# A hybrid decoder trunk on one core: more output units inside the last attention rounds, one query unit moved, row norms broadcast without a diagonal matrix

## What is computed

```python
def rmsnorm(x, g):
    y = x * rsqrt(mean(x * x, axis=-1) + 1e-6)
    return y * g

for i in range(2):
    hn = rmsnorm(x, norm_mix_pre[i])
    m = mamba2_mixer(hn, ...) if i == 0 else diff_attention(hn, ...)
    x = x + rmsnorm(m, norm_mix_post[i])
    hn = rmsnorm(x, norm_ffn_pre[i])
    x = x + rmsnorm(conv_ffn(hn, ...), norm_ffn_post[i])

def diff_attention(u, w_qkv, ..., w_out):      # per head: q, k of 2 x 64, v of 128
    sc = q @ k.T * scale - slope * dist        # causal, two score matrices a head
    a = softmax(sc)[0] - lam * softmax(sc)[1]
    out = rmsnorm(a @ v, subln_g) * (1 - lambda_init)
    return out @ w_out                         # 1024 x 1024
```

## Time and profile before

| | us |
|---|---|
| median of 3 runs | 1522.05 |
| lowest, highest | 1521.98, 1523.62 |
| profiled execution, its own time | 1520.41 |
| its span, first to last instruction | 1518.4 |

### The profile page before, as it was taken

One profiled execution on the slowest core, in us unless ns is written; L12 is line 12 of the kernel. 1 busy time (PEld: TensorE's weight loads), 2 busy tenths in 40 slices (PEclk: granted clock), 3 DMA queues, 4 the chain that ended last, 5 costly groups with the idle time before them and its releaser, 6 DMA issues.

```text
span 1518.4 us, 20441 instructions
## 1 busy us (share of the span) xinstructions
PE 1460.5 (96%) x6774; PEld 1162.1 (77%) x6774; DVE 1021.9 (67%) x1428; ACT 613.2 (40%) x953; POOL 192.4 (13%) x123
## 2 busy tenths in 40 slices
PE   6999999999998999999999999999789999999996
PEld 5778888888786788888888767776568888888885
DVE  6888898889427787778422667778357877776223
ACT  5654555557324323322322436565443332233221
POOL 3011100111113000000011332222121000000111
PEclk9999999999999999999999999999889999999998
DMA  4433323332221222223322121111121322223221
GB/s 150 156 125 124 138 98 137 124 138 70 84 90 63 98 97 86 94 97 105 103 95 86 54 70 56 69 55 55 42 97 56 97 97 97 95 87 112 95 95 55
DMA packets 36277, 142.10 MB, mean 94 GB/s; under 512 B 4048, under 2 KB 4176, under 8 KB 34192
## 3 DMA queue, kind: packets, MB, share of 16 engines
q1 hardware_dynamic: 36240, 141.62, 27.1%
HBM read 139.38 MB, written 2.23 MB: 93 GB/s over the span
## 4 chain that ended last, share of the span: by engine, by line
PE 75%; issue 10%; DVE 7%; POOL 3%; ACT 3%; DMA 1%; DVEq 0%; SPq 0%; POOLq 0%; ACTq 0%
PE bank L395 17%; PE bank L396 16%; PE bank L397 16%; PE b_x L395 6%; PE b_x L397 6%; PE b_x L396 6%; POOL w_lo L350 3%; DVE w_lo L358 1%; DVE cv_s L812 1%; PE b_y L828 1%; ACT w_hi L344 1%; PE b_y L395 1%; PE b_y L396 1%; PE b_y L397 1%; PE b_x L840 1%
## 5 line engine op out<-in xcount | busy, mean ns | idle before, releaser
L358 DVE TENSOR_TENSOR w_lo<-raw,w_hi 128x1024 fp32r<-128x1024 f32 (+1 forms) x190 | 254.4, 1339 | 290.4 <-ACT w_hi L344 290.2
L344 ACT ACTIVATE w_hi<-raw 128x1024 fp32r<-128x1024 f32 (+1 forms) x211 | 233.5, 1107 | 467.1 <-PE bank L397 332.3
L395 PE MATMUL bank<-hn_hi,w_hi 128*128 128x512 f32 x872 | 352.8, 405 | 15.0 <-DVE hn_lo L615 10.8
L396 PE MATMUL bank<-hn_lo,w_hi 128*128 128x512 f32 x872 | 346.8, 398 | 0.0
L397 PE MATMUL bank<-hn_hi,w_lo 128*128 128x512 f32 x872 | 346.7, 398 | 0.0
L395 PEld LDWEIGHTS bank<-hn_hi,w_hi 128*128 128x128 f32 x872 | 165.2, 189 | 58.3 <-issue 12.7
L397 PEld LDWEIGHTS bank<-hn_hi,w_lo 128*128 128x128 f32 x872 | 165.2, 189 | 40.0
L396 PEld LDWEIGHTS bank<-hn_lo,w_hi 128*128 128x128 f32 x872 | 165.4, 190 | 37.8
L395 PE MATMUL b_x<-hn_hi,w_hi 128*128 128x512 f32 x362 | 143.4, 396 | 0.0
L397 PE MATMUL b_x<-hn_hi,w_lo 128*128 128x512 f32 x362 | 143.2, 395 | 0.0
L396 PE MATMUL b_x<-hn_lo,w_hi 128*128 128x512 f32 x362 | 143.1, 395 | 0.0
(11 more groups left out here) (248 smaller groups left out, 2120.1 us busy)
## 6 DMA issues: line engine op xcount, KB each, us to landing
raw<-w_up SPq DMA_DIRECT2D x88, 512.0 KB, 3.2
raw<-w_mix SPq DMA_DIRECT2D x49, 512.0 KB, 3.3
raw<-w_dn SPq DMA_DIRECT2D x32, 704.0 KB, 4.0
raw<-w_qkv SPq DMA_DIRECT2D x24, 512.0 KB, 3.3
acs_bc<-scratch SPq DMA_DIRECT2D x8, 1024.0 KB, 5.3
ecs_bc<-scratch SPq DMA_DIRECT2D x8, 1024.0 KB, 4.7
raw<-w_sout SPq DMA_DIRECT2D x16, 512.0 KB, 3.3
raw<-w_aout SPq DMA_DIRECT2D x8, 512.0 KB, 3.4
```

The source lines that it names most:

```text
L344: nc.scalar.activation(halves_of(ph, rep, first and j < 2)[0], raw[:, slot, 0:ph.width], ACT.Copy).then_inc(hi_made, 1)
L358: nc.vector.tensor_tensor(lo, raw[:, slot_of(ph, rep), 0:ph.width], hi.bitcast(F32), ALU.subtract).then_inc(lo_made, 1)
L395: nc.tensor.matmul(acc[:], wh, hi, start=first, stop=False)
L396: nc.tensor.matmul(acc[:], wh, lo, start=False, stop=False)
```

## The change

Line numbers of the new kernel are a few higher: L403 to 405 are the old L395 to 397, L1345 is L1322, L424 is L416, L458 and L460 are L450 and L452.

1. **Norms without a diagonal matrix**: where a norm isn't split (pre and post norms at the boundaries, 8 of them), DVE stops after the reciprocal. PE makes four matmuls of 128x128 instead of one of 128x512: weights are a column of `rcol`, repeated 128 times by a step of zero, and the moving operand is the identity.
2. **QKV unit 6** (the query unit of round 2) is issued in round 1, between t0 and t1. PE's rounds 2 and 3 are written out (`plain=4`), its loop has two passes instead of three.
3. **AOUT units 0 to 3 in the rounds.** Single steps (j, c), unit j by tile c, take the place of the pairs. Units 2 and 3 have their halves in `ax_hi`, `ax_lo` and accumulate in `b_x`. Their splits are in round 8: ACT's two `split_hi`, POOL's two `split_lo` (DVE did them after the rounds). After the rounds come six steps, then units 4 and 5 written out, then the loop for 6 and 7.

```diff
@@ halves_of
+            if first and ph is AOUT and j in (2, 3):
+                return ax_hi[:, j - 2, 0:ph.width], ax_lo[:, j - 2, 0:ph.width]
@@ split_hi
+            if ph is AOUT and first and j in (2, 3):
+                act.wait_ge(unit_done, QKV.U0 + 4)
+            elif ph is AOUT and first and j in (4, 5):
+                act.wait_ge(unit_done, U - 3)
@@ norm_diag
+            if not split:
+                nc.vector.reciprocal(rcol[:], root[:]).then_inc(diag_ready, 1)
+                return
...
-            else:
-                on_diagonal(diag, rcol[:]).then_inc(diag_ready, 1)
@@ norm_bcast
-                nc.tensor.matmul(b_norm[:], ones[:], diag[:].rearrange("p b t -> p (b t)"),
-                                 start=True, stop=True).then_inc(bc_ready, 1)
+                for b in range(NB):
+                    last = nc.tensor.matmul(b_norm[:, b * P:(b + 1) * P], rcol[:, b:b + 1].to_broadcast([P, P]),
+                                            ident[:], start=True, stop=True)
+                last.then_inc(bc_ready, 1)
@@ out_phase
+            elif ph is AOUT:
+                ahead(split, eng, AOUT, 4, 4)
+                chunk(0, 0, 1)
+                ahead(split, eng, AOUT, 5, 5)
+                for m in range(1, 4):
+                    chunk(m, m % 2, m + 1)
                 body(eng, ph, 2, split, chunk)
@@ in place of aout_start
+        def aout_step(pe, j, c):
             if c == 0:
+                pe.wait_ge(lo_made, AOUT.U0 + j + 1)
+                if j < 2:
                     wait_bank(pe, AOUT, j)
+                else:
+                    pe.wait_ge(s_taken, 4 * NH - 1)
             pe.wait_ge(olo_ready, c + 1)
+            last = product(aout_acc(j), 0, c, o_hi[:, c, :], o_lo[:, c, :], c == 0, c == KC - 1,
+                           halves_of(AOUT, j, True))
+            if c == KC - 1:
+                last.then_inc(unit_done, 1)
@@ att_pe
+            def fill(last_but_one=(), in_last=()):
                 if not proj:
+                    for j, c in in_last if late else last_but_one:
+                        aout_step(pe, j, c)
...
-            if proj and not (started or starting):
+            if proj and not (started or starting or isinstance(h, int) and h == 2):
                 in_unit(pe, QKV, 3 * h, rep)
...
-            filler(4 if late else 0)
+            fill([(0, 0), (0, 1)], [(0, 4), (1, 4)])
...
-            filler(5 if late else 1)
+            fill([(1, 0), (1, 1)], [(0, 5), (1, 5)])
...
-            filler(6 if late else 2)
+            fill([(0, 2), (1, 2)], [(0, 6), (1, 6)])
...
-            if not late:
-                filler(3)
+            fill([(0, 3), (1, 3), (2, 0), (2, 1)], [(3, 0), (3, 1), (3, 2), (2, 3)])
             if two:
                 norm_bcast(pe, norm_no["head"] + h - 2, split=True)
+            fill([(2, 2)], [(2, 4), (3, 3), (2, 5), (3, 4), (3, 5)])
+            if starting:
+                in_unit(pe, QKV, 3 * h + 3, rep + 3)
             if one:
                 weights_back(1, "t1", h - 1)
@@ att_act, after the copy of t2 and after probs(1)
+            if isinstance(h, int) and h == NH:
+                split_hi(act, AOUT, 2, 2)
...
+            if isinstance(h, int) and h == NH:
+                split_hi(act, AOUT, 3, 3)
@@ att_pool
+                if isinstance(h, int) and h == NH:
+                    split_lo(eng, AOUT, 2, 2)
+                    split_lo(eng, AOUT, 3, 3)
@@ DVE
-            out_phase_dve(dve, AOUT, 3, UP1)
+            out_phase_dve(dve, AOUT, 3, UP1, first=4)
@@ PE
-            att_rounds(pe, att_pe)
-            aout_start(pe, KC - 1)
-            with pe.Fori(1, KC // 2) as i:
+            att_rounds(pe, att_pe, plain=4)
+            for j, c in ((0, 7), (1, 7), (2, 6), (2, 7), (3, 6), (3, 7)):
+                aout_step(pe, j, c)
+            for j in (4, 5):
...
+            with pe.Fori(3, KC // 2) as i:
```

63 lines of the change are left out of this document (32 added, 31 removed).

## The result

| | before | after |
|---|---|---|
| median | 1522.01 us | 1505.64 us |
| lowest to highest | 1521.87 to 1523.62 | 1503.59 to 1506.77 |
| profiled execution | 1520.41 us | 1503.59 us |
| its span | 1518.4 us | 1501.8 us |

The ratio is 0.9887, with a 95% interval of 0.9872 to 0.9903: the changed kernel is 16.4 us faster by the medians, where the prediction had 13.5 (1508.5 us). The time lies inside the range. By itself it is nearer to rival (b)'s 1505.4, in which GpSimd costs VectorE nothing, than to the forecast. The traces decide between the two: VectorE was held up as foreseen, and of what the profiled execution gained beyond the forecast most is chance between executions.

What follows compares the result with a forecast made beforehand. TensorE, busy 96% of the span, was taken as the bound. Gains of 3.6 (round 1), 8.4 (rounds 8 and 9) and 1.5 (norms) make 13.5 us off, 1508.5 us against the median, range 1504.5 to 1512.3.

Steps and rivals of the forecast that it cites:

- rival (b): Rounds 8 and 9: GpSimd's low part comes in a gap and costs VectorE nothing; 16.7 us off, 1505.4, chance 0.10.
- Round 1: Moved query unit gains 3.6 us: wait of 2.71 and 1.5 of clock, less 0.6 of new wait.
- Writing out the rounds: TensorE's rounds 2 and 3 as straight code: costed at nothing.
- Round 8: VectorE 1.7 us late through GpSimd's low part, 1.5 us lost to the clock; TensorE's filled waits don't shorten the round.
- The second step of it: Round 8: GpSimd's waiting low part goes ahead of VectorE's second `combine` instruction, which starts at 1053.3 instead of 1051.02.
- Round 9 and AOUT: Filled waits through AOUT unit 3: 11.6 us gained had GpSimd cost nothing, 9.9 with VectorE's delay, 8.4 with the clock.
- rival (e): Rounds 8 and 9: moved steps find operands late and TensorE waits there; a few tenths of a us, no separate chance.
- The fall ahead of the third scores: Round 8: after TensorE's idle 2.6 us ahead of t3 the clock falls to 1.2 GHz, losing 1.5 us.
- Rival (a): Round 8: clock stays up ahead of third scores, or VectorE's second `combine` keeps its turn; 15.0 off, 1507.1, chance 0.25.
- Norms: Eight unsplit norms: 1.8 us gained where scaling waits for the broadcast, 0.3 lost in pre norms; net 1.5.
- The term at the end: End of kernel: first scaling's wait for the broadcast falls from 1.2 to 0.5 us, gaining 0.75.
- Rival (d): Norm matmuls: slow weight loads of a repeated column, 260 ns longer each, make the kernel slower than before; chance 0.02.

Runs made afterwards that it cites:

- the later splits: Changed kernel with the splits of AOUT units 2 and 3 made later, unit 3's in round 9: 1502.74 us, ratio 0.9865; again 1502.88 us, 0.9867.
- the old norms: Changed kernel with the diagonal tile and single broadcast matmul back in the boundary norms: 1507.21 us, ratio 0.9895.
- the earlier scaling: Changed kernel with VectorE's first scalings ahead of the low part of the next phase's unit 3: 1506.51 us, ratio 0.9885.

## Why the prediction was right, and where it was off

**Round 1** was forecast at 3.6 and gave 3.9. The wait for the copy of t1 is 0.47, where 0.91 from t1 to t2 was taken; it is 0.85. The small error is mostly in the unit's own time: the sum put t0's 0.27 ahead of it, but the matmul behind a transpose starts 0.03 after it, so t1 came 5.71 after t0 and not 6.0.

**Writing out the rounds** was costed at nothing; it gives 0.3 in the trace. A jump back of TensorE's loop costs about 0.4 in the one gap where it lies (25.26 against 24.86), which the distances between the norms of the rounds in the trace of before would have shown.

**Round 8** was forecast at 1.7 for VectorE and 1.5 for the clock, 3.2 late, and is 3.1 late. Against the later splits the experiments divide its loss into 1.8 and 1.7, 3.5 in all. The 0.4 between 3.5 and 3.1 is a step that the prediction had wrong: it said that the round keeps its length whatever TensorE gains there, but the filled wait of 0.90 lets t3 come 0.4 earlier and makes the round 0.4 shorter when nothing collides. That the sum came out at 3.1 all the same is two small errors that cancel. This term rested on two rows, the 2.45 us in the earlier trace rows and the precedent in the earlier trace rows. The second step of it, that the engine that waits goes next, came out to the instruction: VectorE's second `combine` began at 1045.06 and by its length stood until about the time when GpSimd ended, 1047.24. The Trainium skill, page "SBUF — State Buffer", section "Who interferes with whom", has a VectorE instruction with two SBUF inputs and a GpSimd instruction that reads SBUF exclude each other for the whole of their length. The 2.72 us agree with that. That it is GpSimd's second low part that costs them is shown by the kernel with the later splits, where the same instruction took 0.75.

**Round 9 and AOUT** were forecast at 11.6 without round 8's delay and gave 12.1. The 0.5 is no more than chance: in the four traces with AOUT as it was, the stretch behind round 9's norm takes 47.77, 47.80, 47.30 and 47.29, in the two of the changed kernel 35.70 and 35.65. Fifteen steps and the broadcast took 11.9 from the statistic to unit 4, where the sum had 12.1. All the operands were there in time, so rival (e) was out.

**The clock.** The fall ahead of the third scores was the right call, but it rested on too little. "The side it is nearest to", between waits of 1.57 and 2.52, happened to be right for 2.30. It held in each of the five traces that have this wait of 2.3 us, the two of the changed kernel and those of AOUT's units only, of the old norms and of the earlier scaling. With the query unit moved alone, waits of 0.90 and of 1.55 with 0.70 and 0.47 were followed by 1.2 GHz as well. Rival (a)'s argument, that 1.57 us idle left the clock alone, was worth nothing as a rule.

**Norms** were forecast at 1.5 and gave 1.0 to 1.5 in the traces, like compared with like. By the medians they are worth 2.2, 0.7 and 2.1 in three pairs, each with an uncertainty of 1.4 us or more. The term at the end was right in size (0.75 forecast, 0.7 measured); the sign for it was described wrongly. The row of the scaling still shows a wait, 1.25 us, because the row counts the idle time from the reciprocal and no longer from the diagonal. Ahead of UP0 0.3 was forecast and 0.2 to 0.4 came. Ahead of QKV nothing was forecast, and nothing is left of the 0.3 of the first table once the clock falls at the same moment. The term that was sized wrong is the one behind AOUT: 0.75 for a wait of 0.90, where the traces have 0.1 in the short form and some 0.4 in the long one.

**The rest.** Between the two profiled executions the gain is 16.8 us, 3.3 more than forecast. 1.1 of it is at the start of the program, where nothing was changed and where the same kernel was 1.0 later on another chip. 0.9 more are at the norms' four places (0.4, 0.3, 1.0 and 0.7 instead of 1.5 in all), because the kernel before had the long form behind AOUT and this execution the short one; the forecast had only the reverse of this among its rivals. 0.5 more are AOUT's, 0.3 round 1's, 0.3 the loop's, 0.1 round 8's, and 0.1 is left with what lies outside the span. So some 2.4 of the 3.3 are chance between two executions. The second profiled execution of the changed kernel gained 14.3, which is 0.8 more than forecast. But the medians are 2.9 and 3.3 beyond the forecast in the two measurements; where they gain it no trace shows, since each measurement has one profiled execution. That the time came out beside rival (b)'s number is no evidence for (b): VectorE's second `combine` took 2.72 us.

**Rival (d)**, a slow load of the repeated column, is out: 190 ns.

## What to carry to other kernels

Before GpSimd gets work beside VectorE, look at what VectorE does at the moment it starts: a low part of 2.4 us put into a dense row of VectorE's cost 3.5 us of the path, and with the splits later it cost nothing that shows. Fill TensorE's idle time where it is waited for, but don't count on the clock staying up behind waits of about 1 us; give it two bounds. And where an engine's work is put first to let another start sooner, ask when the last piece of the row is ready, not the first.

## What the runs showed of the hardware

- The granted clock behind equal waits differed between two kernels that are alike there: 1.00 in one, 0.57 in the other over 4 us, 1.6 us of time for each fall. The work came 3.9 and 2.3 us earlier where the clock fell. What decides it stays open. Behind a wait of 2.3 us it fell in five traces of five.
- At the boundaries the stretch at 1.2 GHz has a shorter and a longer form (granted clock 0.77 and 0.66 over the same 15 us), 1.0 us apart in time, and kernels alike at that place show either. In 36 boundaries the long form came whenever the clock had fallen by 0.4 us after the norm's reciprocal (11), the short one whenever it fell 0.6 us after it or later (25). Differences of that size between two profiles are no evidence for an edit.
- A jump back of TensorE's loop costs about 0.4 us in a row of matmuls that is dense otherwise (25.26 against 24.86 from norm to norm). Writing out the two rounds ahead of the loop gave back 0.28 of it in one place (24.98).
- Weights that are one column repeated by a step of zero load in 190 ns at the median of 64, like the plain 128x128 tiles here.
